# Decoder layer on one core: GpSimd takes twelve low halves, and the feed-forward's splits are reordered

## The reference

```python
h = rms_norm(x, ln1)
u, q, k, v, qi, ki, wi, gates = split(h @ w_in)          # one projection
a_pool = pool_mixer(u)                                   # causal pooling
idx = top_k(indexer_score(qi, wi, ki), 256)              # sparse attention picks 256 keys a query
a_attn = attend(q, k[idx], v[idx], rel_bias)
g = sigmoid(gates)
m = g[:, :D] * (a_pool @ w_pool_proj) + g[:, D:] * (a_attn @ w_attn_proj)
hid = x + m @ w_out
f = rms_norm(hid, ln2) @ w_gate_up
y = hid + (silu(f[:, :F]) * f[:, F:]) @ w_down           # D = 1024, F = 2816
```

## Time and profile before

| | us |
|---|---|
| median of three runs | 1669.35 |
| lowest and highest | 1667.53, 1669.39 |
| the profiled execution | 1668.5 |
| its span in the profile | 1666.8 |

### The profile page before, as it was taken

The page is one execution under the profiler, slowest core; times in us unless marked ns, Lnnn a source line. Parts: engine busy times, 40 slices in busy tenths (PEclk is TensorE's granted clock), DMA queues, the critical chain, the costliest instruction groups (busy, mean ns, idle before and its releaser), DMA issues.

```text
span 1666.8 us, 25440 instructions
## 1 busy us (share of the span) xinstructions
PE 1553.6 (93%) x9345; PEld 1357.2 (81%) x9345; DVE 966.1 (58%) x2237; ACT 519.4 (31%) x1060; POOL 575.7 (35%) x525
## 2 busy tenths in 40 slices
PE   7998999778699988899999699999999999999997
PEld 4553566445598656799899699999999999999997
DVE  2215899992898677323345755555555555545546
ACT  2114211214412555422324523233232242242233
POOL 2001008245244421111111355364364373363450
PEclk9999999899899999999999899999999999999999
DMA  5531011022110001322111121021021021021002
GB/s 169 106 96 51 19 34 32 13 71 69 51 51 26 2 1 39 88 78 64 40 38 39 53 75 52 26 75 50 25 75 50 25 75 50 25 75 45 30 1 115
DMA packets 91043, 87.57 MB, mean 53 GB/s; under 512 B 17215, under 2 KB 81359, under 8 KB 90958
## 3 DMA queue, kind: packets, MB, share of 16 engines
q1 hardware_dynamic: 79591, 73.74, 14.2%
q0 software_dynamic: 3392, 9.97, 2.6%
q10 hardware_dynamic: 7982, 2.83, 0.7%
HBM read 78.30 MB, written 8.45 MB: 52 GB/s over the span
## 4 chain that ended last, share of the span: by engine, by line
PE 56%; issue 2%; DVE 1%; ACT 0%; POOL 0%; POOLq 0%; DVEq 0%
PE banks L1911 27%; PE banks L2008 15%; PE banks L108 13%; DVE yo L2463 0%; PE banks L1868 0%; PE banks L1849 0%; PE banks L2025 0%; POOL wL L2059 0%; ACT XH L2109 0%; ACT sH L2102 0%; ACT resid L2106 0%; DVE hnL_hi L2316 0%; DVE gated L2272 0%; DVE fst L2457 0%; POOL dL L2056 0%
## 5 line engine op out<-in xcount | busy, mean ns | idle before, releaser
L2059 POOL TENSOR_TENSOR wL<-w_raw,wH 128x512 fp32r<-128x512 f32 x176 | 230.0, 1324 | 289.1 <-ACT wH L2152 289.1
L1911 PE MATMUL banks<-hnH,wH 128*128 128x344 f32 x704 | 225.6, 321 | 1.4 <-ACT rinv L2194 0.8
L1911 PE MATMUL banks<-hnH,wL 128*128 128x344 f32 x704 | 224.7, 319 | 0.0
L2450 DVE TENSOR_TENSOR resid<-resid,banks 128x344 f32<-128x344 f32 x264 | 132.0, 511 | 96.8 <-PE banks L2008 96.8
L1369 DVE TENSOR_SCALAR_CACHE_REDUCE pta<-SC,thr 128x384 uint8<-128x384 f32 (+2 forms) x192 | 176.1, 942 | 2.2 <-POOL SC L865 0.2
L2008 PE MATMUL banks<-aH,dH 128*128 128x344 f32 x528 | 169.2, 320 | 0.0
L2008 PE MATMUL banks<-aH,dL 128*128 128x344 f32 x528 | 169.1, 320 | 0.0
L2008 PE MATMUL banks<-aL,dH 128*128 128x344 f32 x528 | 168.2, 319 | 0.0
L1911 PEld LDWEIGHTS banks<-hnH,wH 128*128 128x128 f32 x704 | 132.2, 188 | 2.0 <-issue 1.9
L2152 ACT ACTIVATE wH<-w_raw 128x512 fp32r<-128x512 f32 x176 | 110.0, 626 | 75.1 <-PE banks L1911 62.8
L1911 PEld LDWEIGHTS banks<-hnH,wL 128*128 128x128 f32 x704 | 132.2, 188 | 0.0
(11 more groups left out here) (378 smaller groups left out, 3448.6 us busy)
## 6 DMA issues: line engine op xcount, KB each, us to landing
w_raw<-in_w_gate_up_dram SPq DMA_DIRECT2D x22, 1024.0 KB, 5.2
d_raw<-in_w_down_dram SPq DMA_DIRECT2D x11, 1024.0 KB, 4.9
big<-in_w_in_dram SPq DMA_DIRECT2D x12, 512.0 KB, 3.9
W<-in_x_prompt_dram SPq DMA_DIRECT2D x8, 512.0 KB, 6.9
slab_raw<-in_w_in_dram SPq DMA_DIRECT2D x8, 512.0 KB, 4.0
x_nat<-in_x_prompt_dram SPq DMA_DIRECT2D x8, 512.0 KB, 3.8
slab_raw<-in_w_out_dram SPq DMA_DIRECT2D x8, 512.0 KB, 3.8
out_dram<-yo SPq DMA_DIRECT2D x8, 512.0 KB, 2.6
```

The lines of the kernel that those rows point to most:

```text
L1911: last = mm(out, W_[w][s][:, i * P:(i + 1) * P], x_of(x)(i), start=start and i == 0 and j == 0, stop=stop and i == HALF - 1 and j == 2)
L2059: gp.tensor_tensor(wL[s].rearrange("p (k n) -> p k n", k=HALF), quadrant(x, *HOME[name]), f32(wH[s]).rearrange("p (k n) -> p k n", k=HALF) ...
L2450: V.tensor_tensor(resid[:, m, chunk(DOWN_ORDER[o])], resid[:, m, chunk(DOWN_ORDER[o])], ps[:, 4 + n % 4, 0:CH], ALU.add).then_inc(y_done, 1)
```

## The change

Three pieces are edited.

The first block: `late_splits` and its place after ten rounds are gone from DVE. POOL makes the low halves of units 12 to 23 instead, after the low half of slab 0 and before that of slab 1. ACT's order there is as it was.

The first feed-forward iteration: ACT makes the high halves of S1, S3, S2, S4 of x = 0 and of A11, A12 of x = 1, with the two partial copies between, before the first three silus. The low halves of the second group of T sums go from DVE to POOL, and lie there between the weights' low halves.

Every iteration: the two `w_down` rows are split in the middle of x = 1 instead of within the sums of x = 0, both on ACT (`high_split(g, 2, 0)` and `(g, 2, 1)` around p1 and S1) and on POOL (around S1). `SPLITS` is changed to match, and with it the count that SP waits for.

```diff
@@ -955,6 +954,9 @@
                 low_slab(0)
+                pool.wait_ge(p_ready, PROJ)
+                for u in range(12, 24):
+                    low_x(u)
                 low_slab(1)
@@ -1510,17 +1512,8 @@
-                def late_splits():
-                    dve.wait_ge(p_ready, PROJ)
-                    for u in range(12, 24):
-                        c, k = units[u]
-                        dve.wait_ge(split_hi, u + 1)
-                        V.tensor_tensor(XL[:, k, chunk(c)], hT[:, k, chunk(c)], f32(x_hi[u % 2]), ALU.subtract).then_inc(split_lo, 1)
-
                 dve.wait_ge(mask_ready, 4)
                 for r in range(BITS):
-                    if r == LATE_SPLITS:
-                        late_splits()
                     pair_round(slice(5, 7), (6, 7), r)
@@ -1729,7 +1722,8 @@
-            SPLITS = [(0, "S1"), (2, 0), (0, "S3"), (2, 1), (0, "S2"), (0, "S4")] + [(1, name) for name in SLOTS] + [(3, name) for name in SLOTS[:4]]
+            SPLITS = ([(0, name) for name in SLOTS[4:]] + [(1, name) for name in SLOTS[:4]] + [(2, 0), (1, "S1"), (2, 1)]
+                      + [(1, name) for name in SLOTS[5:]] + [(3, name) for name in SLOTS[:4]])
@@ -2064,14 +2058,28 @@
-                def splits(g, last):
-                    for x, name in ((0, "S1"), (2, 0), (0, "S3"), (2, 1), (0, "S2"), (0, "S4")):
-                        low_split(g, x, name)
+                def low_t(pairs):
+                    for a, j in pairs:
+                        pool.wait_ge(t_hi, 8 + T_SPLIT.index((a, j)) + 1)
+                        if a < 3:
+                            pool.wait_ge(t_made, 12 + T_COUNT[2 * a, j])
+                        gp.tensor_tensor(T_lo[a][2 + j], T_raw[a][2 + j], f32(T_hi[a][2 + j]), ALU.subtract).then_inc(t_lo, 1)
+
+                def splits(g, first, last):
+                    for n, name in enumerate(SLOTS[4:]):
+                        low_split(g, 0, name)
+                        if first and n < 2:
+                            low_t(T_SPLIT[4 + 2 * n:6 + 2 * n])
                     for name in SLOTS[:4]:
                         low_split(g, 1, name)
-                    for n, name in enumerate(("S1", "S3", "S2")):
-                        low_split(g, 1, name)
-                        low_activation(g, n)
+                    low_split(g, 2, 0)
+                    low_split(g, 1, "S1")
+                    low_split(g, 2, 1)
+                    low_activation(g, 0)
+                    low_split(g, 1, "S3")
+                    low_activation(g, 1)
+                    low_split(g, 1, "S2")
+                    low_activation(g, 2)
                     low_split(g, 1, "S4")
@@ -2085,9 +2093,11 @@
                 for name in SLOTS[:4]:
                     low_split(0, 0, name)
-                with pool.Fori(0, NPAIR - 1) as g:
-                    splits(g, False)
-                splits(NPAIR - 1, True)
+                low_t(T_SPLIT[:4])
+                splits(0, True, False)
+                with pool.Fori(1, NPAIR - 1) as g:
+                    splits(g, False, False)
+                splits(NPAIR - 1, False, True)
@@ -2208,24 +2218,31 @@
                     if not first:
                         copy_part(g, 0, "p1")
                     high_split(g, 0, "S1")
-                    silu(g, 0)
-                    high_split(g, 2, 0)
-                    silu(g, 1)
+                    if not first:
+                        silu(g, 0)
+                        silu(g, 1)
                     high_split(g, 0, "S3")
                     copy_part(g, 0, "p4")
-                    high_split(g, 2, 1)
                     high_split(g, 0, "S2")
-                    silu(g, 2)
+                    if not first:
+                        silu(g, 2)
                     high_split(g, 0, "S4")
                     copy_part(g, 0, "p5")
-                    for name in SLOTS[:3]:
+                    if first:
+                        high_split(g, 1, "A11")
+                        high_split(g, 1, "A12")
+                        for n in range(3):
+                            silu(g, n)
+                    for name in SLOTS[2 if first else 0:3]:
                         high_split(g, 1, name)
                     silu(g, 3)
                     high_split(g, 1, "A21")
                     silu(g, 4)
                     silu(g, 5)
+                    high_split(g, 2, 0)
                     copy_part(g, 1, "p1")
                     high_split(g, 1, "S1")
+                    high_split(g, 2, 1)
                     high_activation(g, 0)
@@ -2351,12 +2368,11 @@
                 low_normed(KD * NCH - 1)
                 make_t(1, T_GROUP[2:])
-                low_t(1, T_SPLIT[:4])
@@ -2418,7 +2434,6 @@
                 def invert_norms():
-                    low_t(1, T_SPLIT[4:])
                     for c in (2, 0, 1):
```

More of the change, by code:

```diff
@@ L382, in decoder_layer @@
             EARLY_ROUNDS = 23
-            LATE_SPLITS = 10
             LATE_FROM = 16
@@ L2338, in make_t, with low_t @@
                             V.scalar_tensor_tensor(T_raw[a][k], r22 if a == 2 else r21, l2, T_raw[a // 2][k], ALU.mult, ALU.subtract).then_inc(t_made, 1)
-                def low_t(group, pairs):
+                def low_t(pairs):
                     for a, j in pairs:
-                        dve.wait_ge(t_hi, 8 * group + T_SPLIT.index((a, j)) + 1)
+                        dve.wait_ge(t_hi, T_SPLIT.index((a, j)) + 1)
                         if a < 3:
-                            dve.wait_ge(t_made, 12 * group + T_COUNT[2 * a, j])
-                        V.tensor_tensor(T_lo[a][2 * group + j], T_raw[a][2 * group + j], f32(T_hi[a][2 * group + j]), ALU.subtract).then_inc(t_lo, 1)
+                            dve.wait_ge(t_made, T_COUNT[2 * a, j])
+                        V.tensor_tensor(T_lo[a][j], T_raw[a][j], f32(T_hi[a][j]), ALU.subtract).then_inc(t_lo, 1)
                 residual(0)
@@ L2353, in _ @@
                     if n >= 21:
-                        low_t(0, T_SPLIT[(0, 3, 6)[n - 21]:(3, 6, 8)[n - 21]])
+                        low_t(T_SPLIT[(0, 3, 6)[n - 21]:(3, 6, 8)[n - 21]])
                     if n == KD * NCH - 2:
```

## The result

The changed kernel took 1660.52 us in the median of 9 runs (1656.54 to 1664.03), the kernel before 1669.35 of 9 (1665.50 to 1673.12). The ratio is 0.9949, interval 0.9933 to 0.9965: faster by 8.8 us, where 16 were forecast. The time lies inside the predicted range, near its upper end, at rival (b)'s 1660. The profiled execution is the fastest of the nine: 1656.54 us with a span of 1654.8. One of the six executions of the changed kernel in the last comparison (e11) took 8677.63 us at a mean granted clock of 0.164; it is left out of the median given there.

The account below looks back on a forecast made before the run. TensorE was taken as the bound, busy 93% of the span and never idle in the loop, so gains come from its holes: -12.1 (first block) - 10.3 (first iteration) + 7 (loop) = -15.4 from 1668.5, so 1653 us, range 1643 to 1663.

Parts of the forecast that it names:

- rival (b): First block: DVE's rounds or TensorE's lower clock eat most of part one, leaving 5 to 7 us; 1660 us, chance 0.12.
- Both holes: TensorE's idle waits: 14.99 us in the gates' first slab, 12.02 us before S3's product in the first feed-forward iteration.
- the start of the chain: Gates' first slab: ACT free for keep_x at 425.39, after four copies from 424.60; slab 1 then entered at 439.85.
- part one: First block: twelve low halves on POOL instead of DVE bring attention's minimum 12.1 us earlier; 14.4 or 9 as alternatives.
- The path through TensorE and POOL: First block to attention's minimum: POOL's path would allow 521.8, 14.4 us earlier than the 536.17 before.
- the search: DVE's rounds before attention's minimum: done at 523.7, 524.1 with the settling, so DVE becomes the bound there.
- Part two: First feed-forward iteration: x = 1 starts 13.3 us earlier, less losses within x = 1; 10.3 us gained, bounds 8 to 13.
- the wait for p1: First iteration, x = 1: partial copy p1 done at 956.6, TensorE needs the bank at 954.7; 1.9 us lost.
- that for S3 of x = 1: First iteration, x = 1: the collision of part three costs about 1 us here too.
- Part three: Feed-forward loop: w_down splits in x = 1 cost 0.7 us an iteration, 7 us over ten; bounds 0 and 1.3 each.
- The turns: Loop, x = 1: DVE's four sums and POOL's rows alternate; fourth sum done at 1103.1 instead of 1098.84.
- The three lates: Loop, x = 1: S3's product 0.2 to 0.3 us late, the next two slots 0.26 late each; 0.7 an iteration.

Follow-up runs that it names:

- e11: The changed kernel run again unaltered, for a second profile and for comparison on one chip: 1655.15 us, ratio 0.9956 to the kernel before.
- e4: The changed kernel with the w_down splits of iterations 2 to 11 back in x = 0: 1649.92 us, ratio 0.9898 to the kernel before.
- e2: The kernel before with only the first feed-forward iteration changed: 1660.63 us, ratio 0.9950.
- e3: The kernel before with only the w_down splits moved from x = 0 to x = 1, in all eleven iterations: 1677.19 us, ratio 1.0050.
- e5: The changed kernel with POOL's w_down low halves cut to 8 columns instead of 1024 in iterations 2 to 11: one run, 1652.27 us.
- e6: The changed kernel with DVE's four sums of x = 1 adding 2 columns instead of 128 of each quadrant's rows: one run, 1650.57 us.
- e7: The changed kernel with the two w_down rows split before A22 and A21 of x = 1, all iterations: 1648.93 us, ratio 0.9909 to the kernel before.
- e10: The same kernel as e4, run again beside the changed kernel on one chip: 1651.66 us, ratio 0.9924 to the kernel before.

## Why the prediction was right, and where it was off

**The signs and the mechanisms held.** Both holes closed, and the loop paid for it. The sum was -12.1 - 10.3 + 7 = -15.4; with the parts as measured at the clock that most profiles show, it is -7.4 - 10.4 + 8.7 = -9.1, and the medians gave -8.8.

**The step that failed is the start of the chain in part one:** "ACT is free for `keep_x` at 425.39, after the four copies from 424.60." That row belongs to an execution in which TensorE ran its small matmuls at full clock. Of 13 profiles 11 show them at the lower one: 14 to 15.2 us instead of 8.1. Behind them the copies, and behind these the whole chain, were 5.2 us late. From there on each step fits with that shift: slab 1 at 445.05 against 439.85 + 5.2, the minimum at 526.93 against 521.8 + 5.2. The path through TensorE and POOL, priced at 14.4 us, fell behind the search (523.6 against a predicted 524.1), and the gain to the minimum became 7.4 instead of 12.1. At full clock the chain is where the prediction had it: in e4 slab 1 came at 23.49 us for 23.48, and the gain is 11.5. The low clock's 7.1 us come off the 14.4 of TensorE's path, and 7.3 are left. The kernel before hid this: by e2 and e3 its stretch takes 119.80 us at either clock. The gain therefore varies with the clock, 11.5 or 7.4, and the one profile of before could not show it. Rival (b) had the price, 5 to 7, for the lower clock and a later slab 0, but from gaps inside the slab. The clock had fallen before it, and the cost came through ACT's queue. That the median landed on (b)'s 1660 is therefore partly luck: part one gave 7.4 instead of (b)'s 5 to 7, and the loop's larger loss made up the rest.

**Part two** came out at 10.4 against 10.3, partly because errors cancelled: S3 started 19.8 us after the iteration's start (predicted 19.1) and x = 1 at 26.7 (predicted 26.2). Then x = 1 lost 2.4 us where 2.9 had been priced: the wait for p1 was 0.51 instead of 1.9, that for S3 of x = 1 0.88 (predicted about 1), and S2 and S4 lost the rest.

**Part three** was mis-sized by a fifth: 0.89 us an iteration instead of 0.7, in all 8.7 instead of 7. The turns came as worked out: the fourth sum ended 11.9 us after the start of x = 1 (predicted 12.0). The three lates are 0.30, 0.23 and 0.25, in sum 0.78. The prediction's own steps (0.2 to 0.3, and twice 0.26) add to about 0.77, which it rounded down to 0.7. So x = 1 takes 21.38 us instead of 20.60, and the term left out is 0.11 us in what follows it (22.93 instead of 22.82 to the next iteration), spread over the down products; its cause is not known. The eight sums of an iteration took 1.33 us in the mean, as forecast (near 1.3); the 0.94 set beside it was that of x = 1 alone, and all eight had 0.81 before. With e5, e6 and e7 the cause is shown from both sides: take away either partner of the meeting, or its time, and 64.19 is back.

The Trainium skill, SBUF — State Buffer, section "SBUF: two separate sides", has the port pair of DVE and GpSimd as an exclusive lock for a whole instruction, and only against DVE operations with two SBUF inputs or in a two-port mode. The runs agree on both halves: a 128x8 sum took 2.37 us behind a POOL row (e6), and products with one input in PSUM lost nothing beside a 2.40 us row (e7).

## What to carry to other kernels

A hole in the busiest engine absorbs a delay ahead of it that is shorter than the hole (here 6 to 7 us in one of 15); once it is closed, the start of the chain that replaces it has to be priced at both clock levels, and everything in the queues ahead of it (here four tiny copies on ACT) counts. Work that is moved should be laid beside what the other engine does at that time, not beside its idle time alone: the same two POOL rows cost 0 us before A22 and 0.9 around S1, because only there DVE read two inputs from SBUF. In a loop without idle time count matmuls per 100 us, since a busy share of 100% hid gaps of 0.2 us here.

## What the hardware showed that was not expected

TensorE's clock at one place of the program differed between executions of the same code: 1.00 from 415 to 430 in the kernel before and in e4, whose kernel ran at 0.50 there when taken again (e10); 0.50 (the lower level, 1.2 GHz) in the others from some point between 410 and 421 on. From 410 to 415 TensorE was busy 3.29 of 5 us before, 4.64 in e4, and 2.66 in the changed kernel; but it was busy 4.65 in e3 too, and there the clock fell just behind 420. What decides it was not tested. A group of 32 small matmuls that ran wholly at the lower clock took 7.1 us, although TensorE was busy throughout, and 3.8 at full clock.

The smallest sum (128x8) takes 0.16 us alone (e6's first one) and 2.37 behind POOL: for such a meeting the size of DVE's operation does not matter, only what POOL has left.
